# Summing expert rows in memory by accumulating transfers, pairing two products in one matmul for narrow experts, and moving the last norm's sums to ScalarE

## The chip, the cores and the metric

The kernel runs on one core of one Trainium2 chip. The metric is the device time of one execution in microseconds (us): 4533.25 us before the change, the median of three runs (4527.98 to 4533.9). TensorE multiplies, VectorE, ScalarE and GpSimd do elementwise work, SyncE (SP) issues transfers. In the profile they are PE (PEld for its weight loads), DVE, ACT, POOL and SP. Matmul results go to PSUM, whose banks hold 512 fp32 columns on 128 partitions; everything else is in SBUF (on chip) or DRAM.

## The reference

One decoder layer on 2048 tokens of 1024 features, all float32: a layer norm, one input projection, a pooling mixer beside a sparse attention, an output projection with a residual and a layer norm, then a mixture of 32 experts of which each token takes 4, and a last residual and norm. The change touches the part from the experts on:

```python
top_logit, top_e = lax.top_k(xf @ w_router + b_router, 4)
gates = softmax(top_logit)
order = argsort(top_e.reshape(-1)); tok = order // 4         # rows sorted by expert
hu = ragged_dot(xf[tok], w_gate_up, group_sizes) + b_gate_up[e_sorted]
gate = minimum(hu[:, :1024], 7.0); up = clip(hu[:, 1024:], -7.0, 7.0)
act = (up + 1.0) * gate * sigmoid(1.702 * gate)
y = ragged_dot(act, w_down, group_sizes) + b_down[e_sorted]
ffn = zeros.at[tok].add(y * g_sorted[:, None])
out = layer_norm(2.0**0.25 * h + ffn, ln2_g, ln2_b)          # h: after the first norm
```

With these inputs the experts get between 131 and 356 rows each: 356, 338, 337, 329, 309, three of 300, 297, 285, 277, 272, 269, 268, 267, 261, 258, 252, 249, 246, 239, 235, 227, 227, 209, 207, 202, 200, 193, 185, 167 and 131.

## The kernel before

Five stages follow each other with a barrier between them: `project_stage` (L83, to about 640 us), `attend_stage` (L676, to 1840), `place_stage` (L1651, to 1854), `experts_stage` (L1792, to 4387) and `combine_stage` (L2257, to the end).

While tokens are routed, `weigh` (VectorE, in attend) turns each token's expert and rank into an index, and GpSimd writes the token number there into `lists` in DRAM, by indirect transfers. `place_stage` sorts the experts into visits by their number of rows: each visit handles up to 384 rows of one expert, rounded up to a class of `WIDTHS` (384, 368, ..., 240, in steps of 16). Here there are 32 visits, one per expert, widest first; each class has its own TensorE loop.

A visit has two phases on TensorE, `up` and then the rest, called "down" below. The operands are float32, split into a high part and a low rest that both pass as fp32r, so a product is three matmuls (`passes`, L1995): high by high, high by low, low by high. `up` walks four chunks of gate and up weights; per chunk it makes two blocks of 128 gate features and 128 up features, 8 contraction steps each: 4 x 2 x 2 x 8 x 3 = 384 matmuls as wide as the visit. `up_chunk` (L2007) waits for the low parts of the chunk's weights (`s_lo`) and for free PSUM (`s_gu`). Then come transposes of the next visit's rows (`transpose_x`, L1985; the first waits until all three gathers have landed, `s_x`) and, between them, the down products: for each half of the output features two tiles of 128 rows by 512 features, 24 matmuls each (`down_tile`), and a third tile, a smaller form of it (`down_rest`, `down_few`), or nothing (L2056) for the rows past 256.

The other engines work in a fixed order of their own:

- SP loads weights in 1 MB halves of 2 MB chunks (`chunk`, L1888 and L1893), six chunks a visit, through three buffers, and stores the third row tile in small pieces (`store_third`, L1915 and L1919).
- ScalarE makes the high parts of weights (`high`, L2190) and of rows (L2194), the sigmoid (L2198), the high part of the activations (`high_act`, L2202), and copies finished tiles out of PSUM and issues their store into `y` (`store`, L2209 and L2212).
- VectorE makes the low parts of weights (`low`, L2106) and rows (L2111), and carries each block out of PSUM: bias and clamp (`out_of_psum`, L2117 to L2126) and the product with the sigmoid (`activate`, L2132).
- GpSimd begins a visit by reading the next visit's list (L1958) and gathering its rows by three indirect transfers (`gather`, L1964); then it makes the low part of each of the eight activation blocks (L1972, L1973).

`combine_stage` gathers, for each of 16 tiles of 128 tokens, the four expert rows of each token from `y` by four indirect transfers (L2327). TensorE sums them with the gates as a small matrix (L2369) on top of gates times `b_down` (L2362). VectorE adds the residual (L2397), makes the norm's sums (L2400 to L2405) and applies it in three passes (L2410 to L2415); GpSimd raises to the power of −1/2 (L2343).

Of the kernel before, what the change touches and what calls it, by code (L numbers as in the profile page):

```python
# [18 lines left out]
F32 = mybir.dt.float32  # L19
# [44 lines left out]
WIDTHS = tuple(range(ROWS, 2 * P - 17, -GRAIN))  # L64
# [3 lines left out]
SHORT = WIDTHS.index(2 * P + REST)  # L68
SHORTER = WIDTHS.index(2 * P + FEW)
MAX_VISITS = EXPERTS + SEQ * TOP_E // ROWS  # L70
META = MAX_VISITS + 1
TAIL = 8 * P
CHUNK = 4096
CUT = P // TOP_E
# [8 lines left out]
def project_stage(nc, A, S, D_):  # L83
# [7 lines left out]
    CLEARS = 12  # L91
    SHARE = (MAX_VISITS - EXPERTS) * ROWS // CLEARS
    SHARE_N = next(n for n in range(1, SHARE + 1) if SHARE % n == 0 and SHARE // n <= P)
    assert SHARE * CLEARS == (MAX_VISITS - EXPERTS) * ROWS
# [64 lines left out]
    with ExitStack() as ctx:  # L159
# [23 lines left out]
        zeros = sb("zeros", [P, P])  # L183
# [60 lines left out]
        s_clear = sem("p_clear")  # L244

        with nc.Block() as block:
# [68 lines left out]
            def _(pool):  # L315
# [30 lines left out]
                nc.gpsimd.memset(zeros[:], 0.0)  # L346
# [234 lines left out]
            def _(act):  # L581
# [6 lines left out]
                def out_of_q(t, g):  # L588
# [15 lines left out]
                    else:  # L604
# [6 lines left out]
                        if t >= CLEARS:  # L611
                            return
                        shape = [SHARE // SHARE_N, SHARE_N * D // P, P]
                        row = EXPERTS * ROWS + t * SHARE
                        nc.scalar.dma_start(D_["y"][row:row + SHARE, :].rearrange("(p n) (c d) -> p (n c) d", n=SHARE_N, d=P),
                                            zeros[0:shape[0]].unsqueeze(1).broadcast_to(shape)).then_inc(s_clear, 16)
# [56 lines left out]
                act.wait_ge(s_clear, 16 * CLEARS)  # L673


def attend_stage(nc, A, S, D_):  # L676
# [6 lines left out]
    CLEARS = 16 * 2  # L683
# [201 lines left out]
    with ExitStack() as ctx:  # L885
# [50 lines left out]
        at_i, token = S["at_i"], S["token"]  # L936
# [78 lines left out]
        with nc.Block() as block:  # L1015
            @block.sync
            def _(sp):
# [41 lines left out]
                for g in range(POOL_GROUPS):  # L1059
# [7 lines left out]
                sp.dma_start(D_["lists"][0:EXPERTS * SEQ, :].rearrange("(p n) o -> p (n o)", p=P),  # L1067
                             res[:, 0:EXPERTS * SEQ // P].bitcast(I32)).then_inc(s_clear, 16)
                sp.dma_start(D_["lists"][EXPERTS * SEQ:, :].rearrange("(p n) o -> p (n o)", p=P),
                             res[:, 0:TAIL // P].bitcast(I32)).then_inc(s_clear, 16)  # L1070
# [24 lines left out]
                def transpose(k, n):  # L1095
                    if n:
                        return
                    b = ORDER[k]
                    sp.wait_ge(s_h1, k + 1 + (k == TILES - 1))
                    sp.dma_start(D_["h1"][b * P:(b + 1) * P, :], h1[:]).then_inc(s_h1st, 16)  # L1100
# [3 lines left out]
                sp.wait_ge(s_h1st, 16 * TILES)  # L1104
# [1417 lines left out]
```

## Time and profile before

| | us | share of the span |
|---|---|---|
| median of three runs | 4533.25 | |
| profiled execution, its span | 4529.3 | 100% |
| PE busy | 4289.9 | 95% |
| PEld busy (beside PE) | 3153.5 | 70% |
| DVE busy | 3076.1 | 68% |
| ACT busy | 1817.6 | 40% |
| POOL busy | 1010.1 | 22% |

No other time of the profiled execution is listed than its span. Transfers moved 665.72 MB, 147 GB/s over the span. A busy share is an average over stages; what limits a stage is read in windows of it. In the rows below a time in brackets is the engine's idle time ahead of the instruction, and the name behind the arrow is what ended it; "x3" says that three instructions of one kind stand in one row. In a group's row the first number after the bar is the busy time, the second the mean in ns, the third the idle time ahead of the group's instructions.

### The profile page before, as it was taken

What the parts mean: (1) busy time and instruction counts of PE and PEld (TensorE: products, weight loads), DVE (VectorE), ACT (ScalarE), POOL (GpSimd) and SP (SyncE); (2) the same over time, 40 slices, a digit from 0 to 9 for tenths busy, and PEclk for the clock granted to TensorE, in tenths of its full rate; (3) what the DMA queues carried; (4) which work ended last, traced back from release to release, by engine and by line L of the source; (5) the groups of instructions that cost most, each with busy time, mean ns of one, the idle gap of its engine ahead of it and who ended that gap; (6) DMA issues with size and microseconds to landing.
All of it is one profiled execution on the core that took longest, in us unless ns stands there. A gap on an engine that the chain in (4) does not pass through costs nothing. (4 is left out here: it accounts for less than half of the span.)

```text
span 4529.3 us, 70549 instructions
## 1 busy us (share of the span) xinstructions
PE 4289.9 (95%) x24356; PEld 3153.5 (70%) x24356; DVE 3076.1 (68%) x4861; ACT 1817.6 (40%) x2677; POOL 1010.1 (22%) x1152
## 2 busy tenths in 40 slices
PE   8999988999999998699999999999999999999987
PEld 4444434444444454599989889899999999999961
DVE  2587867878888873555556556666676777777768
ACT  1222223443434433233434444444445555555530
POOL 1111101221111122211112212222222222222235
PEclk9999989999999999799999999999999999999986
DMA  6443330120110010544555456474657667667668
GB/s 194 126 122 92 87 101 16 30 27 21 18 23 16 14 27 19 148 158 148 174 168 190 155 183 220 162 250 161 237 197 239 208 230 241 219 234 237 212 214 362
DMA packets 534140, 665.72 MB, mean 147 GB/s; under 512 B 64416, under 2 KB 402592, under 8 KB 533952
## 3 DMA queue, kind: packets, MB, share of 16 engines
q1 hardware_dynamic: 419664, 501.02, 34.7%
q10 hardware_dynamic: 87744, 77.15, 5.4%
q0 software_dynamic: 26576, 85.56, 5.0%
q8 instruction: 87, 1.43, 0.1%
q14 instruction: 69, 0.57, 0.0%
HBM read 543.61 MB, written 120.03 MB: 147 GB/s over the span
## 5 line engine op out<-in xcount | busy, mean ns | idle before, releaser
L2000 PE MATMUL gu<-x_hi,w_hi 128*128 128x240 f32 (+8 forms) x4096 | 1196.5, 292 | 4.1 <-issue 4.1
L2003 PE MATMUL gu<-x_lo,w_hi 128*128 128x240 f32 (+8 forms) x4096 | 1195.5, 292 | 0.5 <-issue 0.5
L2004 PE MATMUL gu<-x_hi,w_lo 128*128 128x240 f32 (+8 forms) x4096 | 1194.1, 292 | 0.0
L2106 DVE TENSOR_TENSOR w_lo<-w_raw,w_hi 128x2048 fp32r<-128x2048 f32 x386 | 874.6, 2287 | 414.1 <-ACT w_hi L2190 386.2
L2190 ACT ACTIVATE w_hi<-w_raw 128x2048 fp32r<-128x2048 f32 x386 | 726.8, 1908 | 207.4 <-PE gu L2004 132.0
L2000 PEld LDWEIGHTS gu<-x_hi,w_hi 128*128 128x128 f32 x4096 | 774.7, 189 | 4.5 <-issue 4.3
L2003 PEld LDWEIGHTS gu<-x_lo,w_hi 128*128 128x128 f32 x4096 | 773.3, 189 | 1.1 <-issue 0.9
L2004 PEld LDWEIGHTS gu<-x_hi,w_lo 128*128 128x128 f32 x4096 | 773.8, 189 | 0.0
L1972 POOL TENSOR_TENSOR a_lo<-up,a_hi 128x384 fp32r<-128x384 f32 x256 | 396.6, 1549 | 1177.8 <-ACT a_hi L2202 1177.8
L570 PE MATMUL proj_acc<-w_in_sb,hT 128*128 128x512 f32 (+1 forms) x1280 | 499.0, 537 | 0.7 <-ACT hT L586 0.7
L2000 PE MATMUL yp<-w_hi,a_hi 128*128 128x512 f32 x1088 | 445.6, 410 | 2.3
L2003 PE MATMUL yp<-w_lo,a_hi 128*128 128x512 f32 x1088 | 431.4, 397 | 0.0
L2004 PE MATMUL yp<-w_hi,a_lo 128*128 128x512 f32 x1088 | 431.1, 396 | 0.0
L570 PEld LDWEIGHTS proj_acc<-w_in_sb,hT 128*128 128x128 f32 x1280 | 213.9, 192 | 221.4 <-issue 215.7
L2117 DVE TENSOR_SCALAR gate<-gu,b_gu 128x384 f32<-128x384 f32 x256 | 157.3, 614 | 279.0 <-PE gu L2004 278.8
L2202 ACT ACTIVATE a_hi<-up 128x384 fp32r<-128x384 f32 x256 | 134.5, 525 | 384.5 <-DVE up L2132 384.5
L2198 ACT ACTIVATE sig<-gate 128x384 f32<-128x384 f32 x256 | 132.7, 518 | 313.3 <-DVE gate L2117 312.5
L1212 DVE TENSOR_SCALAR_CACHE_REDUCE reach<-scores_odd,small 128x1792 bf16<-128x1792 f32 (+3 forms) x128 | 248.7, 1943 | 9.5 <-issue 1.1
L2000 PEld LDWEIGHTS yp<-w_hi,a_hi 128*128 128x128 f32 x1088 | 205.2, 189 | 64.9 <-POOL a_rest L1973 11.9
L1388 PE MATMUL qk<-kT,q_blk 128*128 128x512 f32 (+3 forms) x480 | 225.2, 552 | 19.4 <-ACT probs L1556 7.7
L2209 ACT ACTIVATE y_rows<-yp 128x512 f32<-128x512 f32 x192 | 113.9, 593 | 322.8 <-PE yp L2004 272.5
L1245 DVE TENSOR_REDUCE small<-qk 128x1 f32<-128x256 f32 (+15 forms) x96 | 123.6, 1288 | 172.3 <-PE qk L1390 170.9
(316 smaller groups left out, 5878.6 us busy)
## 6 DMA issues: line engine op xcount, KB each, us to landing
w_raw<-w_gate_up SPq DMA_DIRECT2D x258, 1024.0 KB, 7.6
w_raw<-w_down SPq DMA_DIRECT2D x128, 1024.0 KB, 8.1
y_dram<-y_rows ACTq DMA_DIRECT2D x128, 256.0 KB, 2.6
y_dram<-zeros ACTq DMA_DIRECT2D x12, 2688.0 KB, 15.5
h_blk<-h_dram SPq DMA_DIRECT2D x32, 512.0 KB, 8.7
qi_dram<-qi_stage ACTq DMA_DIRECT2D x16, 640.0 KB, 3.2
x_in<-x SPq DMA_DIRECT2D x16, 512.0 KB, 6.1
w_in_sb<-w_in SPq DMA_DIRECT2D x4, 2048.0 KB, 14.2
```

Source lines behind the costliest of these rows:

```text
L570: mm = nc.tensor.matmul(acc[:, (5 * t + n) % ACCS, 0:width], hT[:, t % 2, k], w_in[:, k, c0:c0 + width], start=(k == 0), stop=(k == KD - 1))
L1212: nc.vector.tensor_scalar(out, row, limit, 0.0, ALU.is_ge, ALU.add, accum_out=n_reach)
L1388: nc.tensor.matmul(out[:, at:at + width], q[:, k % 2, i], S["kT"][:, i // REP, at:at + width], start=True, stop=False)
L1972: nc.gpsimd.tensor_tensor(a_lo[:, j], up[:, j % 2], a_hi[:, j].bitcast(F32), ALU.subtract)
L2000: op = nc.tensor.matmul(out, s_hi_, m_hi, start=(n == 0), stop=False)
L2003: nc.tensor.matmul(out, s_hi_, m_lo, start=False, stop=False)
L2004: op = nc.tensor.matmul(out, s_lo_, m_hi, start=False, stop=(n == len(pairs) - 1))
L2106: nc.vector.tensor_tensor(w_lo[:, c % 2, cols], raw[:, c % 3, cols], w_hi[:, c % 2, cols].bitcast(F32), ALU.subtract).then_inc(s_lo, 1)
L2117: nc.vector.tensor_scalar(g, gu[:, j % 2, 0, 0:ROWS], S["b_gu"][:, j, bass.ds(e, 1)], LIMIT, ALU.add, ALU.min).then_inc(s_gm, 1)
L2190: nc.scalar.activation(w_hi[:, c % 2, cols], raw[:, c % 3, cols], ACT.Copy).then_inc(s_hi, 1)
L2198: nc.scalar.activation(sig[:, j % 2], gate[:, j % 2], ACT.Sigmoid, scale=SWI_ALPHA).then_inc(s_sig, 1)
L2202: nc.scalar.activation(a_hi[:, j], up[:, j % 2], ACT.Copy).then_inc(s_ah, 1)
```

## The change

- `WIDTHS` become 384, 352, 320, 304, 288, 272, 256, 240, 208 and 176. Each visit takes the narrowest class that holds its rows.
- In visits of at most 256 columns the high rows and the low rows lie side by side (`x_both`). A step of `up` is then two matmuls: the weights' high part by both, into the two halves of a PSUM bank, and their low part by the high rows, into the first half. ScalarE copies the second half to SBUF (`second_sums`), VectorE adds the two halves with the bias. VectorE and ScalarE get a second loop for these visits and work on 256 columns in place of 384.
- The lists hold pairs of a token and its gate. A finished tile is multiplied by the gates while ScalarE copies it out of PSUM, and GpSimd adds it to `sums` in DRAM by indirect transfers that accumulate (`scatter`, seven a visit). `sums` starts as a copy of the first norm's output, stored twice in attend. The array `y`, its zero-filling in the project stage, the piecewise stores on SP and the positions for the later gathers go.
- GpSimd's order in a visit: the last scatter of the visit before at the start; before block 2 it waits until all scatters of the visit before have landed, before block 3 it takes the gates and reads the next list, before blocks 4, 5 and 6 it issues one gather each; the scatters follow after block 7.
- SP reads the list of the third tile in four pieces, and a table of places, before chunk 5 of the visit before (`load_third`), once GpSimd has reached block 3 (`s_hold`).
- `combine_stage` loads `sums` tile by tile, eight ahead. VectorE adds gates times `b_down` from PSUM and applies the norm in two fused passes; ScalarE makes the norm's sums in two accumulating passes; GpSimd makes the power. The weights by expert are made on VectorE at the end of the last visit (`weigh_experts`).

```diff
-WIDTHS = tuple(range(ROWS, 2 * P - 17, -GRAIN))
+WIDTHS = (384, 352, 320, 304, 288, 272, 256, 240, 208, 176)
...
+                def load_third(v):
+                    at = look_up(sp, v, 1, MOST)
                     rest, few = (look_up(sp, v, what, 1) for what in (2, 3))
+                    if not first(v):
+                        sp.wait_ge(s_hold, v)
                     for i in range(4):
+                        row = at + 2 * P + i * FEW - rest * ((i - i % 2) * FEW) - few * (i % 2 * FEW)
+                        sp.dma_start(third[i * FEW:(i + 1) * FEW], D_["lists"][bass.ds(row, FEW), :]
+                                     ).then_inc(s_third, 16)
+                    sp.dma_start(spot[:], A["spots"][bass.ds(rest + few, 1)].rearrange("o p j n -> (o p) j n")
+                                 ).then_inc(s_third, 16)
...
                     for c in range(6):
...
+                        if c == 5:
+                            load_third(v + 1)
                         chunk(v, c, e)
...
+                def gather(v, m):
+                    if m == 0:
+                        pool.wait_ge(s_who, 16 * v + 16)
+                        nc.gpsimd.tensor_tensor(who_now[:], who[:, :, 0], zero[:], ALU.add)
+                        pool.drain()
+                    nc.gpsimd.indirect_dma_start(
+                        x[:, m], None, D_["h1"], bass.IndirectOffsetOnAxis(ap=who_now[:, m:m + 1], axis=0)
+                    ).then_inc(s_x, 16)
...
+                def hold_places(v):
+                    if not first(v):
+                        pool.wait_ge(s_yst[0], 32 * v)
+                        pool.wait_ge(s_yst[1], 32 * v)
+                        pool.wait_ge(s_yst[2], 32 * v)
+                        pool.wait_ge(s_yst[3], 16 * v)
+                    pool.wait_ge(s_third, 80 * v + 80)
...
+                def hold_gates(v):
+                    nc.gpsimd.tensor_copy(gate_now[:, 0:2], who[:, 0:2, 1].bitcast(F32))
+                    nc.gpsimd.tensor_copy(gate_now[:, 2:3], third[:, 1:2].bitcast(F32))
+                    nc.gpsimd.tensor_tensor(at_third[:], scaled[:], spot[:, :, 1], ALU.add).then_inc(s_hold, 1)
+                    pool.drain()
...
+                def scatter(v, n):
+                    pool.wait_ge(s_y, 6 * v + n + 3)
+                    nc.gpsimd.tensor_tensor(idle[:, n:n + 1], zero[:, 0:1], zero[:, 0:1], ALU.add)
+                    if n % 3 < 2:
+                        parts = [(halves, at_main[:, n % 3, n // 3:n // 3 + 1], y[:, n % 3])]
+                    elif n == 2:
+                        parts = [(quarters, at_third[:, w:w + 1], y[:, 2, w * BANK // 2:(w + 1) * BANK // 2])
+                                 for w in range(2)]
+                    else:
+                        parts = [(halves, at_third[:, 2:3], y[:, 2])]
+                    for rows, at, part in parts:
+                        nc.gpsimd.indirect_dma_start(rows, bass.IndirectOffsetOnAxis(ap=at, axis=0), part, None,
+                                                     compute_op=ALU.add).then_inc(s_yst[3 if n == 5 else n % 3], 16)
                 def body(v):
-                    gather(v + 1)
+                    if not first(v):
+                        scatter(v - 1, 5)
                     for j in range(J):
+                        if j == 2:
+                            hold_places(v)
+                        elif j == 3:
+                            hold_gates(v)
+                            list_rows(v + 1)
+                        elif 4 <= j < 7:
+                            gather(v + 1, j - 4)
                         pool.wait_ge(s_ah, 8 * v + j + 1)
                         nc.gpsimd.tensor_tensor(a_lo[:, j], up[:, j % 2], a_hi[:, j].bitcast(F32), ALU.subtract)
                         nc.gpsimd.tensor_copy(a_rest[:, j], up[:, j % 2, 2 * P:2 * P + REST]).then_inc(s_al, 1)
+                    for n in range(5):
+                        scatter(v, n)
...
+                def two_sums(bank, width, triples):
+                    out = bank.rearrange("p (s n) -> p s n", s=2)[:, :, 0:width]
+                    for n, (w_high, w_rest, moving) in enumerate(triples):
+                        nc.tensor.matmul(out, w_high, moving, start=(n == 0), stop=False)
+                        op = nc.tensor.matmul(out[:, 0], w_rest, moving[:, 0], start=False, stop=(n == len(triples) - 1))
+                    return op
...
+                            if width <= 2 * P:
+                                op = two_sums(gu[:, jj, h], width,
+                                              [(hi[:, k, h, cols], lo[:, k, h, cols], x_both[:, :, k, 0:width])
+                                               for k in range(KD)])
+                            else:
+                                op = passes(gu[:, jj, h, 0:width],
+                                            [(hi[:, k, h, cols], lo[:, k, h, cols], x_hi[:, k, 0:width],
+                                              x_lo[:, k, 0:width]) for k in range(KD)])
+                            op.then_inc(s_g1, 1)
...
-                def out_of_psum(v, j, e):
+                def out_of_psum(v, j, e, parted):
                     g, u = gate[:, j % 2], up[:, j % 2]
...
+                    if parted:
+                        g, u = g[:, 0:2 * P], u[:, 0:2 * P]
+                        dve.wait_ge(s_sig, 24 * v + 3 * j + 1)
+                        nc.vector.scalar_tensor_tensor(g, gu[:, j % 2, 0, 0:2 * P], b_gate, g, ALU.add, ALU.add)
+                        dve.drain()
+                        nc.vector.tensor_scalar(g, g, LIMIT, None, ALU.min).then_inc(s_gm, 1)
+                        dve.wait_ge(s_g1, 16 * v + 2 * j + 2)
+                        dve.wait_ge(s_sig, 24 * v + 3 * j + 2)
+                        nc.vector.scalar_tensor_tensor(u, gu[:, j % 2, 1, 0:2 * P], b_up, u, ALU.add, ALU.add
+                                                       ).then_inc(s_gu, 1)
+                        dve.drain()
+                        nc.vector.tensor_scalar(u, u, LIMIT, -LIMIT, ALU.min, ALU.max)
+                        dve.drain()
+                        nc.vector.scalar_tensor_tensor(u, u, 1.0, g, ALU.add, ALU.mult)
+                        return
...
+                def second_sums(v, j):
+                    act.wait_ge(s_g1, 16 * v + 2 * j + 1)
+                    nc.scalar.activation(gate[:, j % 2, 0:2 * P], gu[:, j % 2, 0, 2 * P:], ACT.Copy).then_inc(s_sig, 1)
+                    act.wait_ge(s_g1, 16 * v + 2 * j + 2)
+                    act.wait_ge(s_al, 8 * v + max(j - 1, 0))
+                    nc.scalar.activation(up[:, j % 2, 0:2 * P], gu[:, j % 2, 1, 2 * P:], ACT.Copy).then_inc(s_sig, 1)
...
                 def store(v, n):
...
+                    if n == 0:
+                        act.wait_ge(s_hold, v + 1)
+                    nc.scalar.activation(y[:, slot], yp[:, n % 2], ACT.Copy, scale=gate_now[:, slot:slot + 1]
+                                         ).then_inc(s_y, 1)
...
+                def add_bias(t):
+                    row = total[:, t % AHEAD]
+                    dve.wait_ge(s_in[t % AHEAD], 16 * (t // AHEAD + 1))
+                    dve.wait_ge(s_bias, t + 1)
+                    nc.vector.tensor_tensor(row, row, acc[:, t % SUMS], ALU.add).then_inc(s_tot, 1)
+                def finish(t):
+                    row = total[:, t % AHEAD]
+                    dve.wait_ge(s_square, t + 1)
+                    nc.vector.scalar_tensor_tensor(row, row, column(t, 1), gain[:], ALU.add, ALU.mult)
+                    dve.drain()
+                    dve.wait_ge(s_rstd, t + 1)
+                    nc.vector.scalar_tensor_tensor(row, row, column(t, 4), bias[:], ALU.mult, ALU.add
+                                                   ).then_inc(s_out, 1)
...
+                def spread(t):
+                    row = total[:, t % AHEAD]
+                    act.wait_ge(s_tot, t + 1)
+                    nc.scalar.activation(scratch[:, 0], row, ACT.Copy, accum_out=column(t, 0)).then_inc(s_mean, 1)
+                    act.wait_ge(s_mean, 2 * t + 1)
+                    nc.scalar.activation(column(t, 1), column(t, 0), ACT.Copy, scale=-1.0 / D).then_inc(s_mean, 1)
+                    act.wait_ge(s_mean, 2 * t + 2)
+                    wait(act, s_square, t)
+                    nc.scalar.activation(scratch[:, 1], row, ACT.Square, bias=column(t, 1), accum_out=column(t, 2)
+                                         ).then_inc(s_square, 1)
```

## Rows read from the trace of the kernel before

**Rows 1.** Windows: us, PE, PEld, DVE, ACT, POOL busy, PEclk, DMA share, GB/s.
```profile
640.00:1840.00 1200.00, 1091.83 (x4989) 551.26 (x4989) 898.81 (x1622) 471.23 (x957) 235.71 (x306) 0.96 0.13 28
...
1856.00:4381.00 2525.00, 2502.63 (x16982) 2299.98 (x16982) 1655.70 (x1938) 1189.43 (x1354) 588.80 (x678) 0.99 0.60 201
...
4381.00:4529.00 148.00, 99.94 (x337) 25.89 (x336) 104.76 (x131) 3.67 (x7) 88.12 (x81) 0.63 0.89 352
```

**Rows 2.** Timeline of PE, two visits: start, us, engine, line, operation.
```profile
2952.60 0.37 PE L2000 MATMUL gu<-x_hi,w_hi 128*128 128x272 f32 x1
...
3001.32 0.27 PE L1991 MATMUL e_tr<-ident,x_rows 128*128 128x128 f32 x1
...
3555.71 0.36 PE L2000 MATMUL gu<-x_hi,w_hi 128*128 128x240 f32 x1
...
3599.31 0.27 PE L1991 MATMUL e_tr<-ident,x_rows 128*128 128x128 f32 x1
...
3624.47 0.36 PE L2000 MATMUL gu<-x_hi,w_hi 128*128 128x240 f32 x1
```

**Rows 3.** Groups by line of DVE and ACT, 3600 to 4300 us.
```profile
L2106 DVE TENSOR_TENSOR w_lo<-w_raw,w_hi 128x2048 fp32r<-128x2048 f32 x122 | 276.4, 2286 | 101.3 <-ACT w_hi L2190 101.3
...
L2117 DVE TENSOR_SCALAR gate<-gu,b_gu 128x384 f32<-128x384 f32 x81 | 49.7, 614 | 27.7 <-PE gu L2004 27.7
...
L2126 DVE TENSOR_TENSOR up<-up,gate 128x384 f32<-128x384 f32 x81 | 45.2, 558 | 6.1
...
L2124 DVE TENSOR_SCALAR up<-up 128x384 f32<-128x384 f32 x81 | 29.9, 369 | 8.4
...
L2198 ACT ACTIVATE sig<-gate 128x384 f32<-128x384 f32 x81 | 42.0, 518 | 94.7 <-DVE gate L2117 94.1
```

**Rows 4.** Timeline of DVE in a visit of 240 columns.
```profile
3588.74 0.62 DVE L2117 TENSOR_SCALAR gate<-gu,b_gu 128x384 f32<-128x384 f32 x1 [0.81 <-PE gu L2004]
...
3599.62 0.62 DVE L2117 TENSOR_SCALAR gate<-gu,b_gu 128x384 f32<-128x384 f32 x1 [0.80 <-PE gu L2004]
```

**Rows 5.** Timeline of ACT in that visit.
```profile
3557.41 3.72 ACT L2190 ACTIVATE w_hi<-w_raw 128x2048 fp32r<-128x2048 f32 x2 [1.03 <-issue]
```

**Rows 6.** Timeline of POOL in that visit.
```profile
3557.56 0.95 POOL L1964 DMA_INDIRECT x_rows<-h_dram,who_now  x1 [0.30 <-issue]
...
3594.47 2.44 POOL L1972 TENSOR_TENSOR a_lo<-up,a_hi 128x384 fp32r<-128x384 f32 x1 [4.70 <-ACT a_hi L2202]
```

**Rows 7.** Tile x_rows, visits of 352 and 336 columns.
```profile
DMA to landing us min/median/max: 4.5/5.3/6.4
```

**Rows 8.** Tile x_rows, the later visits.
```profile
DMA to landing us min/median/max: 7.0/7.5/9.5
```

**Rows 9.** DMA issues: count, KB each, median us to landing.
```profile
w_raw<-w_gate_up SPq DMA_DIRECT2D x258, 1024.0 KB, 7.6
...
x_rows<-h_dram,who_now POOLq DMA_INDIRECT x99, 7.5
...
lists_dram<-token,at_i POOLq DMA_INDIRECT x64, 5.9
```

**Rows 10.** Timeline of SP: stores of the third tile.
```profile
3545.94 4.80 SPq L1919 DMA_DIRECT2D y_dram<-y_rows  x8
```

**Rows 11.** Timeline of PE, end of experts and start of combine.
```profile
4380.73 0.30 PE L2056 MATMUL yp<-so_far,ident 128*128 128x32 f32 x2
...
4396.68 3.77 PE L2362 MATMUL c_acc<-b_down_sb,by_expertT 32*128 32x512 f32 x4
```

**Rows 12.** Timeline of POOL, start of combine.
```profile
4387.07 0.10 POOL L2332 MEMSET minus_half<- 128x1 f32 x1 [25.72 <-POOLq L1873]
```

**Rows 13.** Timeline of DVE, last instruction.
```profile
4525.00 1.23 DVE L2415 TENSOR_TENSOR total<-total,bias 128x1024 f32<-128x1024 f32 x1
```

**Rows 14.** Groups of POOL in combine.
```profile
L2327 POOL DMA_INDIRECT rows<-y_dram,pos_by_pick x64 | 74.1, 1157 | 22.8 <-issue 17.6 <-PE c_acc L2369 5.2
```

**Rows 15.** Groups of DVE in combine.
```profile
L2397 DVE SCALAR_TENSOR_TENSOR total<-h_blk,c_acc 128x1024 f32<-128x1024 f32 x16 | 19.5, 1220 | 27.2 <-PE c_acc L2369 26.8 <-DMA out<-total 0.4
```

**Rows 16.** Timeline of POOL, start of experts.
```profile
1853.51 0.21 POOL L1703 TENSOR_SCALAR_AFFINE_SELECT mine<-mine 128x32 f32<-128x32 f32 x1 [6.52 <-issue]
```

More of the change, by code:

```diff
@@ L63 @@
 GRAIN = 16
-WIDTHS = tuple(range(ROWS, 2 * P - 17, -GRAIN))
+WIDTHS = (384, 352, 320, 304, 288, 272, 256, 240, 208, 176)
+KINDS = tuple((ROWS - width) // GRAIN for width in WIDTHS)
+LAST_KIND = tuple(kind - 1 for kind in KINDS[1:]) + KINDS[-1:]
+ONE_SUM = sum(width > 2 * P for width in WIDTHS)
+PEELED = 2
 REST = 64
@@ new lines, in gather @@
+                def gather(v, m):
[13 more added lines that the diff above has]
+                    pool.wait_ge(s_third, 80 * v + 80)
+                    nc.gpsimd.tensor_tensor(scaled[:], spot[:, :, 0], third[:, 0:1].broadcast_to([P, 3]), ALU.mult)
+                    for h in range(2):
+                        nc.gpsimd.tensor_scalar(at_main[:, :, h], who[:, 0:2, 0], 2.0, float(h), ALU.mult, ALU.add)
@@ L1977, in _ @@
                 pool.wait_ge(S["listed"], 64 * TILES)
-                gather(0)
+                list_rows(0)
+                for m in range(3):
+                    gather(0, m)
                 n = over_visits(pool, body)
+                scatter(n - 1, 5)
                 pool.wait_ge(s_x, 48 * n + 48)
-                nc.gpsimd.tensor_tensor(who_now[:], who[:], zero[:], ALU.add)
+                pool.wait_ge(s_yst[0], 32 * n)
+                pool.wait_ge(s_yst[1], 32 * n)
+                pool.wait_ge(s_yst[2], 32 * n)
+                pool.wait_ge(s_yst[3], 16 * n)
+                pool.wait_ge(s_third, 80 * n + 80)
+                nc.gpsimd.tensor_tensor(who_now[:], who[:, :, 0], zero[:], ALU.add)
             @block.tensor
@@ L2316, in _ @@
                     sp.wait_ge(s_out, t + 1)
-                    sp.dma_start(out_dram[t * P:(t + 1) * P, :], total[:, t % OUTS]).then_inc(s_st[t % OUTS], 16)
-                for n in range(OUTS):
-                    sp.wait_ge(s_st[n], 16 * len(range(n, TILES, OUTS)))
+                    sp.dma_start(out_dram[t * P:(t + 1) * P, :], total[:, t % AHEAD]).then_inc(s_st[t % AHEAD], 16)
+                    if t >= 2 and t - 2 + AHEAD < TILES:
+                        load(t - 2 + AHEAD)
+                for n in range(AHEAD):
+                    sp.wait_ge(s_st[n], 16 * len(range(n, TILES, AHEAD)))
```

453 lines of the change are left out of this document (187 added, 266 removed).

## The prediction

> **What bounds the kernel now.** I read the stages first, by windows [rows 1]. TensorE is busy 1092 of 1200 us in the attend stage, 2503 of 2525 in the experts stage and 100 of 148 in the combine stage, where the clock falls to 0.63 and the DMA share is 0.89. So experts go at TensorE's pace and combine at that of its transfers. Then I read one visit on TensorE's timeline [rows 2]. Its first phase ("up", 384 matmuls) lasts 3599.31 − 3555.71 = 43.60 us at 240 columns, the rest ("down": transposes of the next visit's rows, then 512-wide matmuls) 25.16, and the next visit starts at 3624.47: 68.76 in all, with no gap. At 272 columns "up" is 3001.32 − 2952.60 = 48.72. One matmul is then 43.60/384 = 113.5 ns at 240 columns and 126.9 at 272: 0.42 ns per column and a fixed 13.5 ns. Last I read what stands close behind TensorE there: VectorE's groups, its rounds and GpSimd's order [rows 3 to 6].
>
> **Part 1: fewer, wider matmuls in narrow visits.** The new classes put 15 of the 32 visits at 256 columns or less: three at 256, five at 240, five at 208, two at 176 (from three at 256 and twelve at 240; counts of rows per expert from the reference's own routing). There a triple becomes one matmul of 2n columns and one of n. By the line above a triple of 240 is 3 × 113.5 = 340.5 ns now and 480 × 0.417 + 13.5 + 113.5 = 327 after; of 208 about 287, of 176 about 247. With 128 triples per visit TensorE alone would save 1.7 us in a 240 visit, 6.8 at 208, 12 at 176, 1 at 256: 5 × 1.7 + 5 × 6.8 + 2 × 12 + 3 = 70 at most; with the slower pace of long matmuls about 60 to 65. Against it, two visits become 16 columns wider, 2.6 to 3 each: 6.
>
> I don't book the 60, because of VectorE. Its round (two blocks) is 2 × 2.286 for the low parts of the weights, and 2 × (0.614 + 0.61 + 0.369 + 0.558 + 0.56) for the blocks: 10.0 us busy [rows 3] of a round of 3599.62 − 3588.74 = 10.88 [rows 4]. TensorE after needs 9.2 at 208 and 8.0 at 176. The blocks get narrower (256 of 384 columns) but have six operations in place of five, about 9.4 to 9.7 busy, and a new hop: ScalarE copies the second half of each psum bank before VectorE may add it (about 0.4 us, by two thirds of 0.518 [rows 3]). So a round is about 10.5, whatever TensorE could do. ScalarE no longer issues the row stores, so the first weight conversion begins some 0.9 us earlier (it now waits 1.03 for the issue [rows 5]).
>
> In this part a rule of the Trainium skill speaks against the edit. No row shows matmuls closer than 113.5 ns. TensorE: Matmul & The Clock Gate, section "LDWEIGHTS (loading the stationary operand)", gives a load as columns/1.2 ns, 107 ns for 128 columns; a 208- or 176-column matmul (an estimate by the slope: 100 or 87 ns) would not cover it, and the TensorE saving would be some 10 us less. By it rival 3 below would gain that much less.
>
> **Part 2: the third gather.** Now the three gathers of the next visit's rows are issued at the start of a visit, 1.25 us apart, the third at 3557.56, 1.85 us after the visit began [rows 6], and land over 30 us before use. After, they are issued one at a time between GpSimd's own steps, the third only after a_lo(5). In the 240 visit that step begins 38.8 us into the visit and takes 2.44 [rows 6]: it ends 41.2, a_rest 41.4. With the shorter rounds and the earlier start of narrow visits I put the issue at 39.6 to 40.0. TensorE's first transpose waits for all three, so "down" starts at 40 + L instead of 43.6, L being the time from issue to landing. The nearest rows: 4.5 to 6.4 where no weights are on their way [rows 7], 7.0 to 9.5 beside a weight load [rows 8]. At that moment two gathers have landed and the weight loads issued about 11 to 14 us before (two chunks of 2 MB, each half 7.6 us to land [rows 9]) are nearly in, so I take L = 5 to 5.5.
>
> Narrow: 40 + 5.3 + 25.16 ≈ 70.5 to 71 per visit against 68.76: +2.1 to 2.4 for the five of 240, +1.7 for the seven narrower ones, +1.2 for three of 256: 27. Wide: the gather comes three chunks and 9.0 us after the start (the stretch between the last chunk's start and the end of a_lo(5), with GpSimd's three other new steps before it): 36.5 + 9.0 + 5.5 = 51 against 48.72 at 272, +1.9 to 2.4 for six; +1 to 1.9 for two of 288, +0.2 to 0.9 for four of 304, 0 above 320: 16. Sum 43, with 2 more for spots where landings scatter, less the part of the 6 above that hides in them: I take **+45** with the widths. Its ends: L = 4.5 gives +24, L = 7.5 gives +106 (26 of the visits move one for one with L).
>
> **Part 3: accumulated stores.** Seven accumulating scatters per visit on GpSimd (0.95 and 0.30 each, as its gathers [rows 6]: 9 us) lie in "down", where it is idle. The trace has no accumulating transfer; nearest are 5.9 us for scatters and 7.5 for gathers [rows 9]. A slot of ScalarE's copies is needed again about 11 us later (the 25.16 us of "down" hold four row tiles, two of them lie between); up to there a landing costs 0. If the transfer must first read like a gather and then write like a scatter, it is 7.5 + 5.9 = 13.4, 2.4 too long, some 2 us in each of 31 visits: +60. I take 0, as both nearest rows are one transfer, and keep +60 as an end. The thirds' stores on SP (8 issues, 4.80 us [rows 10]) go; five small loads of about 0.6 us each come, before chunk 5, behind a wait for GpSimd's fourth block. Queued behind it are chunk 5 and the next chunk 0; both still land before they are read. 0.
>
> **Part 4: combine.** Now: last matmul 4380.73, GpSimd released 4387.07, end 4529.3: 142.2 us from the release [rows 11 to 13], 7.4 per tile after the start. 64 gathers of 1.157 with 0.36 idle each on GpSimd carry it [rows 14]. After, 512 KB per tile come from the summed rows, and VectorE has an addition and two fused steps of 1.14 to 1.22 (like L2397's 1.220 [rows 15]): about 3.6 per tile, 16 tiles 57.3. ScalarE's two accumulating passes over 1024 columns are unseen; by its 0.518 for 384 columns [rows 3] each is about 1.2, 2.4 to 3 per tile: below VectorE. The first bias matmul now starts 9.6 after the release (4396.68 [rows 11]); constants still set it. So the end is 9.6 + 3.8 + 57.3 + about 3 for the pipeline's depth + 3.0 (from 4525.00 + 1.23 to the span's end [rows 13]) = 76.5. The release comes 3.3 later, as the last accumulations must land. 142.2 − 76.5 − 3.3 = **62.4** saved; 70 if VectorE never waits, 52 if ScalarE or the loads set 4.3 per tile.
>
> **Part 5: small ones.** Start of experts: GpSimd's wait of 6.52 before 1853.51 [rows 16] goes (2.2 of it on the path), five small loads come before the first chunk (3): +1. Attend: two more small VectorE steps for each of 16 tiles beside a busy TensorE: +2 (0 to +5). Project: zero-filling of the row store goes, off TensorE's path: −1 (−1 to 0).
>
> **Sum.** 45 − 62.4 + 1 + 2 − 1 = −15.4. The profiled span is 4529.3, 3.95 below the median 4533.25 and inside the three times, which is all that is given of that execution. 4529.3 − 15.4 = 4513.9; with the same 3.95, **4518**.
>
> **Rivals.** About 9 us (0.2%) either way is what a measurement can tell from no change.
>
> 1. The forecast (0.50), 4495 to 4545: a combine gain of 62, of which late gathers eat three quarters. L may be 4.5 (4497) to 6.2 (4536).
> 2. Gathers land in time (0.13): then narrow visits are limited by VectorE's rounds, about 66.4 at every width, −25 + 6 in place of +45: about **4453**. For it: a single gather may be quicker than three. Against: issue at 40 leaves only 3.6 before 43.6, and no row is below 4.5.
> 3. Narrow visits reach TensorE's bound (0.08): −62 + 6, total −117: about **4416**. Against it, VectorE's 10.0 of 10.88.
> 4. The other side (0.20): the third gather still meets weight loads and takes 7.5 as most do [rows 9]: +106 in experts, +46 in all: **4579**, slower. It decides from L = 5.9 (no net gain) and L = 6.2 (slower by 0.2%); for it, SP's chunk 5 is issued later than now.
> 5. Accumulating transfers read and then write, 13.4 us (0.09): ScalarE's copies wait for their slots, +60 on the forecast, **4578**. The Trainium skill's DMA: Bandwidth & Descriptors, section "Rules for kernel authors", says that such a transfer reads its destination and writes it later; no row of this trace shows one.
>
> That the change does not do what it says is in 2 and 3's failure: the double width removes only 13 ns of a triple at 240, since weight loads already run beside matmuls (PE 2503 against PEld 2300 busy [rows 1]).
>
> Chances: faster by over 0.2%: 0.50 × 0.68 + 0.13 + 0.08 = 0.55. Within: 0.50 × 0.25 and a few hundredths of 4 and 5: 0.17. Slower: the rest, 0.28. The range 4450 to 4578 leaves out rival 3 and half of 4 and 5.
>
> **What would show it.** Right: TensorE's idle time before the transposes ends on the DMA of x_rows, 2 us in most narrow visits; combine is about 77 us from release to end, VectorE full; the first stages unchanged. Wrong: "up" of 176 and 208 far under 40 us (VectorE isn't the bound); no wait before the transposes; ScalarE waiting for the landing of sums; VectorE idle in combine for loads.

## The result, and the profile after

The changed kernel takes 4542.92 us in the median of 20 runs, the kernel before 4532.12 in 20 runs beside them: ratio 1.0025, 95% interval 1.0018 to 1.0031. It is slower, by a quarter of a per cent. The profiled execution has a span of 4541.6 us, 12.3 more than that of before.

Where the 12.3 come from, by the starts of the visits on TensorE's two timelines (after less before):

| stretch | measured | predicted |
|---|---|---|
| start to the first "up" | −1.24 | +2 |
| first four visits, two of them 16 columns wider | +5.86 | +6 |
| visits of 320 to 272 columns (13) | +7.91 | +16 |
| visits of 256 columns (3) | +1.49 | +3.6 |
| visits of 240 columns and less (12) | +55.39 | +23 |
| last matmul of the experts to the end | −57.11 | −62.4 |

The forecast column adds up to −11.8 and not to the −15.4 of the sum, which took 45 for the four rows of visits together (48.6 here), since a part of the 6 should hide in the waits. So combine gave nearly what was forecast, and the twelve narrow visits took it back. First the windows of the changed kernel, experts and combine, with the columns of [rows 1]:

```profile
1856.00:4450.00 2594.00, 2486.96 (x15060) 2239.01 (x15061) 1635.59 (x2054) 1230.23 (x1593) 1171.78 (x1278) 0.98 0.63 196
4450.00:4541.00 91.00, 59.00 (x84) 23.27 (x82) 60.13 (x52) 45.11 (x86) 18.29 (x38) 0.54 0.58 204
```

TensorE, which had hardly a gap in the experts stage [rows 1], now idles 107 us there. The first visit of 240 columns shows where (timeline of the changed kernel, answering to [rows 2, 4 to 6]; the DVE, ACT and POOL rows and the last PE row are from a visit of 208):

```profile
3569.73 0.47 PE L2045 MATMUL gu<-x_both,w_hi 128*128 128x480 f32 x1
...
3616.17 1.11 PE L2025 MATMUL e_tr<-ident,x_rows 128*128 128x128 f32 x4 [3.96 <-DMA x_rows<-h_dram,who_now]
...
3617.51 0.63 PE L2037 MATMUL yp<-w_lo,a_hi 128*128 128x512 f32 x1
3617.93 0.63 PE L2038 MATMUL yp<-w_hi,a_lo 128*128 128x512 f32 x1
...
3621.93 0.40 PE L2034 MATMUL yp<-w_hi,a_hi 128*128 128x512 f32 x1
...
3643.64 0.47 PE L2045 MATMUL gu<-x_both,w_hi 128*128 128x480 f32 x1
...
3959.09 0.48 DVE L2167 SCALAR_TENSOR_TENSOR gate<-gu,b_gu,gate 128x256 f32<-128x256 f32 x1 [0.87 <-ACT gate L2273]
...
3970.07 0.48 DVE L2167 SCALAR_TENSOR_TENSOR gate<-gu,b_gu,gate 128x256 f32<-128x256 f32 x1 [0.87 <-ACT gate L2273]
...
3958.25 0.42 ACT L2287 ACTIVATE a_hi<-up 128x256 fp32r<-128x256 f32 x1 [1.44 <-DVE up L2195]
3958.58 0.37 ACT L2273 ACTIVATE gate<-gu 128x256 f32<-128x256 f32 x1
...
3975.63 2.54 POOL L1996 TENSOR_TENSOR a_lo<-up,a_hi 128x384 fp32r<-128x384 f32 x1 [3.41 <-ACT a_hi L2287]
...
3978.57 0.98 POOL L1945 DMA_INDIRECT x_rows<-h_dram,who_now  x1 [0.16 <-issue]
...
3983.71 0.68 PE L2025 MATMUL e_tr<-ident,x_rows 128*128 128x128 f32 x2 [6.07 <-DMA x_rows<-h_dram,who_now]
```

Three things are to be seen. TensorE is done with "up" 42.5 us into the visit of 240 and waits 3.96 us for the third gather; in the one of 208 it waits 6.07. The visit of 208 began at 3937.39: the third gather is issued 41.2 us into it, and TensorE goes on 5.1 later. And after the wait a 512-wide matmul is followed by the next after 0.43 us (3617.51 to 3617.93) for some 5 us, where 0.235 is its pace otherwise: the clock has fallen. The windows of "up" and "down" of a visit of 256, one of 240 and one of 176 show it in the column PEclk:

```profile
3497.97:3544.66 46.69, 45.09 (x259) 39.03 (x258) 36.49 (x54) 26.15 (x40) 23.91 (x29) 1.00 0.65 212
3544.66:3569.73 25.07, 24.87 (x116) 20.20 (x117) 13.79 (x15) 13.74 (x18) 13.11 (x11) 1.00 0.81 233
3569.73:3616.17 46.44, 42.49 (x259) 38.19 (x258) 36.77 (x55) 25.81 (x40) 24.60 (x29) 0.98 0.65 213
3616.17:3643.64 27.47, 27.27 (x116) 22.11 (x117) 13.41 (x13) 13.74 (x18) 11.61 (x11) 0.90 0.78 212
4303.51:4349.86 46.35, 37.14 (x259) 36.51 (x258) 36.77 (x55) 25.56 (x40) 24.49 (x29) 0.95 0.65 214
4349.86:4377.41 27.55, 27.35 (x117) 22.15 (x117) 13.41 (x13) 13.74 (x18) 11.60 (x11) 0.90 0.77 212
```

"Up" with its wait is 46.3 to 46.6 us in all twelve, whatever their width; "down" is about 26.5 and 27.5 in turn, where it was 25.16. At 256 columns, with 1.6 us of waiting, the clock stays at 1.00 and "down" is 25.07. The accumulating transfers land in time (tile of the sums, whole stage):

```profile
DMA to landing us min/median/max: 3.6/7.2/9.3
```

Combine (timeline of the changed kernel, answering to [rows 11 to 13], then VectorE's groups there, answering to [rows 15]):

```profile
4450.14 0.30 PE L2103 MATMUL yp<-so_far,ident 128*128 128x32 f32 x2
...
4460.56 0.10 POOL L2420 MEMSET minus_half<- 128x1 f32 x1 [1.14 <-POOLq L1878]
...
4470.60 4.63 PE L2444 MATMUL c_acc<-b_down_sb,by_expertT 32*128 32x512 f32 x5 [6.42 <-DMA bias<-ln_b]
...
4474.52 1.22 DVE L2454 TENSOR_TENSOR total<-total,c_acc 128x1024 f32<-128x1024 f32 x1 [22.20 <-PE c_acc L2444]
4477.89 1.22 DVE L2454 TENSOR_TENSOR total<-total,c_acc 128x1024 f32<-128x1024 f32 x1 [2.16 <-PE c_acc L2444]
4481.31 1.22 DVE L2454 TENSOR_TENSOR total<-total,c_acc 128x1024 f32<-128x1024 f32 x1 [2.19 <-PE c_acc L2444]
...
4536.81 1.28 DVE L2462 SCALAR_TENSOR_TENSOR total<-total,small,bias 128x1024 f32<-128x1024 f32 x1
```

```profile
L2462 DVE SCALAR_TENSOR_TENSOR total<-total,small,bias 128x1024 f32<-128x1024 f32 x16 | 20.5, 1284 | 1.2
L2459 DVE SCALAR_TENSOR_TENSOR total<-total,small,gain 128x1024 f32<-128x1024 f32 x16 | 20.4, 1277 | 0.0
L2454 DVE TENSOR_TENSOR total<-total,c_acc 128x1024 f32<-128x1024 f32 x16 | 19.4, 1214 | 26.5 <-PE c_acc L2444 26.5
```

VectorE begins 14.0 us after the release at 4460.56, behind the constants, waits 2.2 us each before the second and third tile, and is busy from then on.

### The profile page after: what moved, and what is told of

It reads as the page before. It is cut to its first block and busy times, and to the rows that moved or that the text cites. A ratio compares the mean times of both kernels' runs of the same rounds, so it can differ in the third digit from the quotient of the medians.

```text
span 4541.6 us, 67559 instructions
## 1 busy us (share of the span) xinstructions
PE 4232.6 (93%) x22180; PEld 3089.4 (68%) x22180; DVE 3013.3 (66%) x4933; ACT 1900.3 (42%) x2996; POOL 1525.4 (34%) x1712
## 5 line engine op out<-in xcount | busy, mean ns | idle before, releaser
L2034 PE MATMUL gu<-x_both,w_hi 128*128 128x272 f32 (+5 forms) x2176 | 665.1, 306 | 11.2 <-DVE x_both L2158 11.2
L2037 PE MATMUL gu<-x_both,w_hi 128*128 128x272 f32 (+5 forms) x2176 | 665.0, 306 | 0.0
L2038 PE MATMUL gu<-x_both,w_lo 128*128 128x272 f32 (+5 forms) x2176 | 663.7, 305 | 0.0
L1996 POOL TENSOR_TENSOR a_lo<-up,a_hi 128x384 fp32r<-128x384 f32 x256 | 383.5, 1498 | 778.1 <-ACT a_hi L2287 777.6
L2045 PE MATMUL gu<-x_both,w_hi 128*128 128x480 f32 (+3 forms) x1920 | 615.0, 377 | 13.1 <-DVE up L2172 13.1
L2046 PE MATMUL gu<-x_both,w_lo 128*128 128x240 f32 (+3 forms) x1920 | 512.7, 267 | 0.0
L2034 PEld LDWEIGHTS gu<-x_both,w_hi 128*128 128x128 f32 x2176 | 411.1, 189 | 11.6 <-issue 11.4
L2038 PEld LDWEIGHTS gu<-x_both,w_lo 128*128 128x128 f32 x2176 | 411.4, 189 | 0.0
L2037 PEld LDWEIGHTS gu<-x_both,w_hi 128*128 128x128 f32 x2176 | 411.0, 189 | 0.2
L2045 PEld LDWEIGHTS gu<-x_both,w_hi 128*128 128x128 f32 x1920 | 361.2, 188 | 53.4 <-DVE up L2172 16.4
L2046 PEld LDWEIGHTS gu<-x_both,w_lo 128*128 128x128 f32 x1920 | 365.0, 190 | 0.0
L1972 POOL TENSOR_TENSOR idle<-zero 128x1 int32<-128x1 int32 x192 | 160.3, 835 | 481.8 <-ACT y_rows L2301 481.8
L2301 ACT ACTIVATE y_rows<-yp,gate_now 128x512 f32<-128x512 f32 x192 | 131.7, 686 | 424.2 <-PE yp L2038 370.4
L2287 ACT ACTIVATE a_hi<-up 128x384 fp32r<-128x384 f32 (+1 forms) x256 | 121.6, 475 | 345.4 <-DVE up L2195 345.4
```

The lines of the kernel that those rows point to most:

```text
L1972: nc.gpsimd.tensor_tensor(idle[:, n:n + 1], zero[:, 0:1], zero[:, 0:1], ALU.add)
L1996: nc.gpsimd.tensor_tensor(a_lo[:, j], up[:, j % 2], a_hi[:, j].bitcast(F32), ALU.subtract)
L2034: op = nc.tensor.matmul(out, s_hi_, m_hi, start=(n == 0), stop=False)
L2037: nc.tensor.matmul(out, s_hi_, m_lo, start=False, stop=False)
L2038: op = nc.tensor.matmul(out, s_lo_, m_hi, start=False, stop=(n == len(pairs) - 1))
L2045: nc.tensor.matmul(out, w_high, moving, start=(n == 0), stop=False)
```

## The experiments

The theory after the result: the narrow visits are held by the third gather, which comes late because VectorE's rounds last 10.98 us, and the wait for it costs clock as well as its own length. The rival: the accumulating transfers and the new copies slow "down" by themselves.

**All gathers before block 4.**

```diff
-                        elif 4 <= j < 7:
-                            gather(v + 1, j - 4)
+                        elif j == 4:
+                            for m in range(3):
+                                gather(v + 1, m)
```

> The changed kernel, with all three gathers of the next visit's rows issued before block 4 (the third some 34 to 36 us into a narrow visit in place of 41.2). Theory (late third gather, and the clock it costs): the wait before the transposes falls from 3.6 to 7 us to under 1 in visits of 240 and under 2 in narrower ones, 'down' of the twelve visits of 240 columns and less returns from 26.4 to 27.5 us to 25.1, those visits take 67 to 68.5 us in place of 73.5, wide visits lose their 1 us of waiting; the run goes from 4543 to 4465 to 4480. Rival (the accumulating transfers and the copies slow 'down' by themselves): 'down' stays at 26.4 to 27.5 and only the wait is gained: about 4500.

Measured: 4504.23 us, ratio to before 0.9939 (0.9922 to 0.9955). 38.7 us are gained, little more than half of what the theory gave; by its time the run is the rival's, so it can't decide between the two. The wide visits and those of 240 lost their wait, and the transposes begin 41.7 to 42.8 us into the narrow ones (in the seven narrowest still after a wait of 1.2 to 2.7), but "down" became longer, 27.6 to 29.6 us in visits of 240 and less. A timeline of this kernel, visit of 240 that began at 3556.61:

```profile
3606.98 0.80 PE L2035 MATMUL yp<-w_hi,a_hi 128*128 128x512 f32 x1 [2.52 <-POOL a_rest L1998]
...
3605.75 1.00 POOL L1997 TENSOR_TENSOR a_lo<-up,a_hi 128x384 fp32r<-128x384 f32 x1 [2.88 <-ACT a_hi L2288]
...
3585.67 0.48 DVE L2168 SCALAR_TENSOR_TENSOR gate<-gu,b_gu,gate 128x256 f32<-128x256 f32 x1
...
3591.51 1.63 DVE L2178 SCALAR_TENSOR_TENSOR up<-up,gate 128x256 f32<-128x256 f32 x1
...
3598.09 0.48 DVE L2168 SCALAR_TENSOR_TENSOR gate<-gu,b_gu,gate 128x256 f32<-128x256 f32 x1
```

The first down tile has come to its eighth step, and the last low part a_lo(7) is only ready 50 us into the visit: behind the gather stood a second wait, on the chain VectorE, ScalarE, GpSimd, and the clock falls in it too (0.94 in "down" in eleven of the twelve narrow visits). A part of it is new: the round in which the three gathers are issued lasts 12.3 to 12.4 us (3585.67 to 3598.09) and not about 11, as one product of VectorE in it takes 1.63 us. In the kernel before the tile came to that step at about the moment when a_lo(7) was ready, 48.9 us in.

**The kernel before, with its third gather late.**

```diff
-                    for m in range(3):
-                        nc.gpsimd.indirect_dma_start(...)
+                    for m in range(3 if first(v) else 2):
+                        gather_one(m)
...
                     for j in range(J):
+                        if j == 6:
+                            gather_one(2)
```

> The kernel before, with its third gather alone moved behind a_lo(5), nothing else changed. Theory: the third gather is issued 41.6 us into a visit of 240 and lands at about 46.9, so 'up' with its wait lasts 46.9 in place of 43.6, and 'down' 26.4 to 27.5 in place of 25.16 because TensorE's clock falls in the wait: +4.9 in twelve visits, about +1.1 in eight of 272 and 288, +0.6 in three of 256: 4532 becomes about 4600. Rival (the wait costs its own length and nothing more): 'down' stays 25.16, 12 x 3.2 + 11 = +49: about 4581.

Measured: 4584.56 us, ratio 1.0115 (1.0098 to 1.0132), +52 us, between the two and nearer to the rival. The gather landed in 4.1 to 4.6 us at that place, so TensorE waited 2.0 to 2.5 us in visits of 240, and the clock fell in every second of them, for 1.4 us each: some 8 of the 52 us. Windows of "up" and "down" of two visits in a row:

```profile
3570.16:3616.29 46.13, 43.76 (x388) 43.57 (x386) 37.81 (x47) 22.88 (x24) 15.03 (x17) 1.00 0.63 214
3616.29:3642.66 26.37, 26.26 (x117) 21.39 (x117) 13.56 (x14) 13.92 (x18) 3.00 (x5) 0.94 0.71 223
3642.66:3688.71 46.05, 43.76 (x388) 43.57 (x386) 37.74 (x47) 22.88 (x24) 14.93 (x17) 1.00 0.63 214
3688.71:3713.66 24.95, 24.84 (x116) 20.20 (x117) 13.55 (x14) 13.92 (x18) 2.95 (x5) 1.00 0.75 235
```

This kernel has no accumulating transfers and no new copies, and its "down" is 26.4 all the same after such a wait: the rival isn't needed for it. The late gather alone costs the kernel before 52 us.

**Three matmuls in every visit** (the pairing taken back, the rest of the change kept).

```diff
-                            if width <= 2 * P:
+                            if width <= 0:
                                 op = two_sums(...)
...
-                with dve.Fori(1, one_sum) as v:
-                    body(v, False)
-                with dve.Fori(one_sum, more + 1) as v:
-                    body(v, True)
+                with dve.Fori(1, more + 1) as v:
+                    body(v, False)
...
```

ScalarE's second loop goes in the same way.

> The changed kernel with the paired products taken back: three matmuls per step in every visit, VectorE and ScalarE in the one loop of wide visits; classes, lists, accumulating stores and combine stay. Theory (VectorE's rounds and the third gather set the narrow visits, not TensorE's matmuls): rounds 10.9, narrow visits within 1 us of 73.5, the run within 15 us of 4543, rather a little faster since TensorE idles less. Rival (the pairing does save TensorE's time): 'up' of the narrow visits gets longer by 1.7 to 7 us and the run is 30 to 60 us slower.

Measured: 4548.44 us (ratio 1.0031, 1.0019 to 1.0044), 5.5 above the changed kernel, with intervals that overlap. With the gather late, the pairing is worth next to nothing: without it the third gather is issued 41.1 to 41.6 us into a narrow visit, as with it (41.2 to 41.7).

**TensorE kept busy in the wait.** Matmuls without use between "up" and the transposes.

```diff
                     up(v, width)
+                    for _ in range(BUSY.get(width, 0)):
+                        nc.tensor.matmul(tr[:, 0, 0:P], S["ident"][:], S["ident"][:], start=True, stop=True)
                     transpose_x(v + 1, 0, tiles)
```

> The changed kernel with 32, 48 and 60 matmuls of 128 columns without use between 'up' and the transposes in visits of 240, 208 and 176 columns, which fill most of TensorE's wait. Theory (idle time before the transposes lowers the clock): the transposes still begin 46.3 to 46.6 us into the visit, 'down' returns to 25.1 to 25.5: 12 x 1.9 = 22 us, 4543 becomes about 4521. Rival (the longer 'down' comes from transfers or copies beside it): no change, 4543 or a little more.

Measured: 4568.85 us. The counts were wrong: one such matmul takes 0.225 us, double of what I had set, so they ran on 2 to 8 us after the gather had landed. "Down" behind them was 25.0 us at full clock in the narrow visits (25.1 in the last), but the time of the run tells nothing. With 15, 26 and 30:

> The changed kernel with 15, 26 and 30 matmuls of 128 columns without use (0.225 us each, by the run with more of them) in visits of 240, 208 and 176, so that TensorE is busy nearly until the gather lands and no longer. Theory (idle time before the transposes lowers the clock): they begin 46.3 to 46.6 us into the visit as without, 'down' returns from 26.4 to 27.5 to 25.1 to 25.4: 12 x 1.8 = 22 us, 4543 becomes about 4521. Rival ('down' is longer for transfers or copies beside it): 4543 stays.

Measured: 4522.75 us, ratio 0.9981 (0.9972 to 0.9991): 20.2 us less than the changed kernel for work without use. A timeline of this kernel in a visit of 208, and the windows of its "up" and "down":

```profile
3971.72 5.98 PE L2111 MATMUL e_tr<-ident 128*128 128x128 f32 x52
3977.94 0.32 PE L2025 MATMUL e_tr<-ident,x_rows 128*128 128x128 f32 x1 [0.24 <-DMA x_rows<-h_dram,who_now]
```

```profile
3931.62:3977.90 46.28, 44.97 (x311) 44.13 (x309) 36.69 (x55) 25.65 (x40) 24.60 (x29) 1.00 0.64 214
3977.90:4003.01 25.11, 24.87 (x116) 20.20 (x117) 13.32 (x13) 13.76 (x18) 13.13 (x11) 1.00 0.81 233
```

The transposes begin no earlier (46.3 us in), and "down" is 25.1 with the clock at 1.00. So it is in eleven of the twelve narrow visits (25.0 to 25.2); in the first of 240, where TensorE still waited 1.9 us, it is 26.6 at 0.94. The longer "down" was the clock. The accumulating transfers are as many here, so the rival falls.

**The gate copy ahead on ScalarE** (with the early gathers).

```diff
-                            second_sums(v, 2 * c)
+                            second_gates(v, 2 * c)
+                            second_ups(v, 2 * c)
                         sigmoid(v, 2 * c, parted)
+                        if parted:
+                            second_gates(v, 2 * c + 1)
                         high_act(v, 2 * c, parted)
```

`second_gates` and `second_ups` are the two halves of `second_sums`; the up copy stays where it was.

> Gathers before block 4 as in the first run, and in narrow visits ScalarE copies the second half of a gate block's sums before the high part of the activations of the block ahead of it, not behind it. Theory (the narrow visits are set by VectorE's rounds of 10.98 us, in which it waits 0.87 us for that copy, and then by the last low part a_lo(7) at 50 us, for which the first down tile waits 2.5 us and loses clock): rounds fall to 10.1 to 10.6, a_lo(7) comes at 47 to 48 us, the wait in the first tile goes or falls under 1 us, visits take 67.5 to 68.5 in place of 70 to 71.6: 4504 becomes about 4465. Rival (VectorE is held up by GpSimd's transfers and low parts, not by the order on ScalarE): rounds stay 10.9, the run stays within 8 us of 4504.

Measured: 4462.69 us, ratio 0.9845 (0.9823 to 0.9866). VectorE's gates in a visit of 208 that began at 3967.49:

```profile
3977.23 0.48 DVE L2168 SCALAR_TENSOR_TENSOR gate<-gu,b_gu,gate 128x256 f32<-128x256 f32 x1
...
3987.77 0.48 DVE L2168 SCALAR_TENSOR_TENSOR gate<-gu,b_gu,gate 128x256 f32<-128x256 f32 x1
```

The wait of 0.87 is gone, the round is 10.54, a_lo(7) ends 46.9 us into the visit, narrow visits take 66.8 to 68.8. One copy in each round moved ahead of one other instruction is worth 41.5 us. Not all of it is the 0.87: the round with the gathers falls from 12.3 to 11.1 us in nine of the twelve narrow visits (12.1 in the others), and why it does isn't shown. TensorE still waits 1.8 to 3.0 us for the gathers in the seven narrowest visits, and in five of them the clock falls.

**Three matmuls with the early gathers.** The edits of the first and the third experiment together.

```diff
+                        elif j == 4:
+                            for m in range(3):
+                                gather(v + 1, m)
...
+                            if width <= 0:
                                 op = two_sums(...)
```

> Three matmuls in every visit (no pairing) with the gathers before block 4. Theory (pairing has lengthened the chain of VectorE and ScalarE, so that it gives nothing once the gathers are early): narrow visits near those of the kernel before, 68.8 to 70, against 70 to 71.6 with pairing; 4475 to 4490 against 4504. Rival (pairing pays once the wait is gone): slower than 4504 by 10 or more.

Measured: 4485.08 us, ratio 0.9896 (0.9874 to 0.9917). So the pairing as it was written costs 19 us once the gathers are early (4504.23), and gains 22 with the better order (4462.69).

**Combine's constants.** TensorE waits for `b_down` alone, VectorE for gain and bias before its first finish.

```diff
-                pe.wait_ge(s_const, 48)
+                pe.wait_ge(s_down, 16)
...
-                dve.wait_ge(s_const, 48)
...
+                    if t == 0:
+                        dve.wait_ge(s_const, 32)
                     dve.wait_ge(s_square, t + 1)
```

> The kernel of the run before, and in combine TensorE waits for b_down alone and VectorE for gain and bias only before its first finish. Theory (combine's start is set by the constants: first bias matmul 10.0 us after the release, first sum 14.0): the first sum comes at 8 to 9 us, the stage ends 5 to 6 us earlier, the rest as VectorE's 3.7 us per tile has it. Rival (the first tile of sums lands no sooner): under 2 us.

Measured: 4457.02 us (ratio 0.9838, 0.9817 to 0.986), 5.7 less than the run before, with intervals that overlap (four executions each, which spread over 9 us). The first sum of this kernel comes 5.6 us after the release at 4379.82; it and the last instruction of VectorE:

```profile
4385.38 1.22 DVE L2460 TENSOR_TENSOR total<-total,c_acc 128x1024 f32<-128x1024 f32 x1 [13.75 <-PE c_acc L2450]
...
4446.32 1.28 DVE L2470 SCALAR_TENSOR_TENSOR total<-total,small,bias 128x1024 f32<-128x1024 f32 x1
```

The first sum came 8.4 us sooner than in the changed kernel, and the waits before the second and third tile are 3.0 in place of 4.35 us. In the profiled executions the stage takes 71.2 us from its release to the end of the span, against 81.0 in the changed kernel and in the run before: 9.8 less, more than the 5 to 6 of the theory.

**The classes 368 and 336 back.** On top of the run before.

```diff
-WIDTHS = (384, 352, 320, 304, 288, 272, 256, 240, 208, 176)
+WIDTHS = (384, 368, 352, 336, 320, 304, 288, 272, 256, 240, 208, 176)
...
```

> Early gathers, ScalarE's order and combine's constants as in the runs before, and the classes 368 and 336 put back beside the new ones. Theory (a visit of over 256 columns costs TensorE's matmuls): the first visit goes back from 384 to 368 columns (2.1 us), the fourth from 352 to 336 (3.4 us), the rest unchanged: 4457 becomes about 4451.5. Rival (two more loops on TensorE cost as much in code): within 2 us of 4457.

Measured: 4448.9 us, ratio 0.9807 (0.9793 to 0.982), median of five executions. The first visit's "up" is 67.97 in place of 69.99 in the run before, the fourth's 58.88 in place of 62.29: 5.4 us, near the 5.5 of the theory. The medians differ by 8.1, with intervals that overlap. This version beats both kernels, by 1.9% and 2.1%.

## Why the prediction was wrong

It forecast a gain of 15 us; the kernel lost 11 by the medians and 12 in the profiled executions. The step that failed is part 2, the price of the third gather in narrow visits: 55 us in the twelve and not 23, by two terms, one too small (10 us) and one missing (22 us).

- "A round is about 10.5" (part 1). It is 10.98, longer than before. I counted VectorE's operations and took the hop through ScalarE as 0.4 us, without asking what stands ahead of the copy in ScalarE's order: it is a_hi of the block before, which waits for VectorE's own product. VectorE idles 0.87 for it. With that the third gather is issued 41.2 to 41.7 us into the visit and not at 39.6 to 40.0, and "up" with its wait is 46.3 to 46.6 in place of 45.3 to 46.0. The row of before gave 41.4 for that place [rows 6]; what I took off for shorter rounds did not come. When the copy moved ahead, the round was 10.54; with the late gathers that order was not run, so how much of the late issue it would have taken away is argued and not shown. That the visits of 208 and 176 gain nothing from TensorE's shorter work was forecast, and the third experiment bears it out.
- "40 + L + 25.16" (part 2). I let "down" keep its 25.16 behind any wait. It takes 26.4 to 27.5, as the clock falls in a wait of 3.6 to 7 us: 12 × 1.8 = 22 us that stood in no term, and 20.2 by the run that kept TensorE busy. A row of combine that I had read, clock 0.63 with TensorE waiting for transfers [rows 1], showed that the clock falls in waits, though not how short a wait does it.
- L itself, 5 to 5.5, was right (5.1). In the wide visits the sum was too high, 16 for 7.9. With those of 256 and the start of the kernel, 13 us came out better than forecast and hid a part of the error.
- Part 4 was right in kind and 5 us too good: the release 4.1 later (3.3), the first sum 14.0 after it (13.4), the rest by VectorE's 3.7 per tile (3.6), with two waits of 2.2 us for TensorE that stood in no term.
- Parts 3 and 5 and the widths were right within 3.3 us. Landings of 3.6 to 9.3 stay under 11, so rival 5 fell.
- Of the rivals the fourth named the right side and the wrong cause: L was not 7.5. The point from which it "decides" left out that the issue could be late as well. Rivals 2 and 3 asked for a gather in time; the first experiment shows that even then a_lo(7) holds the visit, a wait that none of them named.
- Its sign of being right came in kind and not in size: the wait ends on x_rows, but lasts 3.6 to 7 us and not 2, and combine takes 81.0 us from release to end and not 77.
- Two figures don't follow from its own 26 us per us of L: at L = 6.2 the sum gives 4541 and not 4536, at L = 7.5 it gives +102 and not +106. Neither bears on what failed.

Open: why "down" is about 26.5 and 27.5 in turn; no run was made for it.

## What to carry to other kernels

Price a wait of the engine that sets the pace twice: by its length, and by the clock that it gives up. When an operand takes a new way through a second engine, look up what stands ahead of it in that engine's order; here one copy moved ahead of one instruction turned a loss of 19 us into a gain of 22. A part that frees one engine is worth something only when the next chain behind it is shorter too, and taking a wait away shows that chain at once.

## What the runs showed of the hardware

- After waits of 3.6 to 7 us TensorE's matmuls ran at half their pace for 3 to 5 us (0.43 in place of 0.235 us, the 1.2 GHz level). After waits of 1.8 to 3.0 us the clock fell in some visits and not in others (in every second one of the kernel before with its late gather, 2.0 to 2.5 us), after the waits of up to 1.8 in the visits of 256 and more of the changed kernel in none.
- Three matmuls per step come 111.8 ns apart at 208 columns and at 176 alike (42.93 us over 384): "up" is 42.95 and 42.93 us in the run with early gathers and no pairing, with the weight loads busy all the time:

```profile
4256.19:4299.12 42.93, 42.93 (x387) 42.93 (x386) 35.98 (x42) 22.32 (x23) 24.71 (x27) 1.00 0.64 209
```

  This agrees with the Trainium skill (TensorE: Matmul & The Clock Gate, section "LDWEIGHTS (loading the stationary operand)"), which gives a load as its columns divided by 1.2, in ns: an estimate of 107 ns for 128 columns, against 111.8 here. In pairs a step takes 0.27 us at 176 columns, 0.30 at 208 and 0.33 at 240 (medians in the changed kernel), where part 1 had 0.247, 0.287 and 0.327. TensorE's own saving is then some 52 us (an estimate from these steps and the 43.60 and 46.15 us of before) and not 60 to 65, short by about the 10 us that part 1 set against it.
- Accumulating transfers land like gathers, 7.2 us in the median against 7.5 for the gathers of before [rows 9], and not like a gather and a scatter one after the other (13.4), though each moves rows of 2 KB or less and a gather rows of 4 KB.
- In the first experiment one product of VectorE takes 1.6 us and not 0.42 in each of the twelve narrow visits (at 3591.51). It begins 0.3 us before the last of the three gathers in a row ends on GpSimd and ends after the low part that GpSimd makes next. In the changed kernel, where the gathers come one at a time, no such product there is longer than 0.43. Which of GpSimd's two instructions holds it isn't shown.
